# Expert weights as 4 MB pair loads, with filler multiplications on TensorE, in a two-layer hybrid encoder

## What is computed

```python
def hier_moe(h, wg, bg, we, be, w1, w3, w2):       # per layer: 32 experts, 4 groups of 8
    gprob = softmax(t @ wg + bg); gval, gidx = top_k(gprob, 1)
    ...
    for e in range(MOE_EXPERTS):
        he = jax.nn.silu(t @ w1[e]) * (t @ w3[e])  # w1, w3: 1024 x 512
        y = y + gate[:, e:e + 1] * (he @ w2[e])    # w2: 512 x 1024
```

## Time and profile before

| | |
|---|---|
| median of 3 runs | 1262.14 us (1261.61 to 1263.18) |
| profiled execution, its own time | 1262.0 us |
| its span | 1260.1 us |
| mean granted TensorE clock | 0.924 of full speed |
| TensorE busy | 1001.1 us, 79% of the span |
| read from HBM | 457.13 MB, 364 GB/s over the span |

### The profile page before, as it was taken

How to read it: one execution, slowest core, us unless ns; L and a number is a source line. 1 busy time by engine, 2 the same in 40 slices (tenths; PEclk the granted TensorE clock), 3 DMA queues, 4 the chain that set the end, 5 groups by cost and what they waited for, 6 DMA issues and landing times.

```text
span 1260.1 us, 20742 instructions
## 1 busy us (share of the span) xinstructions
PE 1001.1 (79%) x8905; PEld 606.8 (48%) x8905; DVE 334.1 (27%) x992; ACT 178.8 (14%) x393; POOL 18.4 (1%) x20
## 2 busy tenths in 40 slices
PE   9999999757576766667999999999857576666665
PEld 6667466424242424333888775465424242423332
DVE  4895341101010110002747553241101010101001
ACT  2315130000000000001224561030000000000000
POOL 0121000000000000000000000000000000000000
PEclk9999999988887988888999999999979887989889
DMA  9931599999999999999944546679999999999998
GB/s 377 416 135 67 226 400 429 428 427 431 426 430 427 430 427 430 428 428 426 409 171 168 184 151 273 261 294 427 426 430 427 430 427 430 428 430 428 430 426 334
DMA packets 34656, 458.91 MB, mean 364 GB/s; under 512 B 3856, under 2 KB 4656, under 8 KB 7216
## 3 DMA queue, kind: packets, MB, share of 16 engines
q1 hardware_dynamic: 33408, 454.00, 86.2%
q10 hardware_dynamic: 1200, 4.23, 1.0%
HBM read 457.13 MB, written 1.08 MB: 364 GB/s over the span
## 4 chain that ended last, share of the span: by engine, by line
DMA 39%; PE 35%; SPq 16%; DVE 2%; issue 1%; another core or an unknown queue 0%; ACT 0%; DVEq 0%
DMA extra<-in_moe_units 20%; DMA ring<-in_moe_units 19%; SPq L341 16%; PE bank L793 11%; PE bank L685 6%; PE bank L895 4%; PE bank L704 3%; PE bank L598 2%; PE bank L664 1%; PE bank L422 1%; PE bank L716 1%; PE bank L852 1%; PE bank L561 1%; PE bank L643 1%; PE bank L630 1%
## 5 line engine op out<-in xcount | busy, mean ns | idle before, releaser
L685 PE MATMUL bank<-ring,xT 128*32 128x256 f32 x2560 | 185.3, 437 | 83.4 <-DMA ring<-in_moe_units 83.4
L685 PE MATMUL bank<-extra,xT 128*32 128x256 f32 x1536 | 123.5, 475 | 71.8 <-DMA extra<-in_moe_units 71.8
L685 PEld LDWEIGHTS bank<-ring,xT 128*32 128x32 f32 x2560 | 84.4, 119 | 169.1 <-DMA ring<-in_moe_units 96.8
L793 PE MATMUL bank<-h,ring 128*128 128x256 f32 x576 | 130.1, 382 | 0.0
L793 PEld LDWEIGHTS bank<-h,ring 128*128 128x128 f32 x576 | 107.4, 190 | 16.5 <-issue 2.9
L685 PEld LDWEIGHTS bank<-extra,xT 128*32 128x32 f32 x1536 | 53.1, 128 | 128.4 <-DMA extra<-in_moe_units 84.9
L704 PE MATMUL bank<-ring,gates_ 128*32 128x256 f32 x1024 | 73.2, 434 | 42.6 <-DMA ring<-in_moe_units 42.6
L704 PE MATMUL bank<-extra,gates_ 128*32 128x256 f32 x1024 | 71.2, 425 | 35.8 <-DMA extra<-in_moe_units 33.4
L1575 DVE TENSOR_TENSOR hT<-hT,bank 128x128 f32<-128x128 f32 x64 | 18.4, 288 | 254.6 <-ACT hT L1065 254.6
L1065 ACT ACTIVATE hT<-bank 128x128 f32<-128x128 f32 x64 | 17.7, 277 | 449.0 <-PE bank L685 449.0
L716 PE MATMUL bank<-xT,gates_ 128*128 128x256 f32 x256 | 70.2, 407 | 3.8 <-DVE xT L1580 2.2
(11 more groups left out here) (312 smaller groups left out, 899.8 us busy)
## 6 DMA issues: line engine op xcount, KB each, us to landing
ring<-in_moe_units SPq DMA_DIRECT2D x112, 2048.0 KB, 49.1
extra<-in_moe_units SPq DMA_DIRECT2D x80, 2048.0 KB, 49.3
ring<-in_od_in_units SPq DMA_DIRECT2D x10, 2048.0 KB, 32.6
ring<-in_ev_in_units SPq DMA_DIRECT2D x5, 2048.0 KB, 26.5
ring<-in_od_out_units SPq DMA_DIRECT2D x4, 2048.0 KB, 8.1
ring<-in_ev_out_units SPq DMA_DIRECT2D x2, 2048.0 KB, 28.4
hT<-sums ACTq DMA_DIRECT2D x4, 512.0 KB, 4.4
every<-sums ACTq DMA_DIRECT2D x4, 512.0 KB, 5.6
```

The costliest lines, as they stand in the source:

```text
L685: last = mm(bank[4 + e % 2][32 * j:32 * j + 32, 0:256], xT[:, 4 * part + k, CAP * e:CAP * e + CAP], w[:, k, :, 256 * (j // 2) + j % 2:256 ...
L793: last = mm(o, w[:, k, P * q:P * q + P], (h2 if u else hT)[:, k, :], start=(k == 0), stop=(k == KT - 1))
```

## The change

In the experts' loop on SyncE, which loads steps 2 to 7 of each layer, units 0 to 9 come as five pairs, each one issue of 128 partitions x 8192 floats (4 MB). In HBM a pair now lies partition by partition, 32 KB in a row. Units 10 and 11 stay alone. Steps 0 and 1 still load unit by unit, from the new layout: 16 KB rows that are 32 KB apart. A pair reports on the semaphore of its even unit, so that unit waits for both, and the odd one waits for nothing new. A pair is issued once both its units are used. To lie side by side, `extra3` and `extra4` are cut from one tile, `extra2` and `extra0` from another, and units change places; `FREED` keeps the order in which places are filled in step 0. TensorE waits for `pt_ok` ahead of unit 2, no longer ahead of unit 8, and multiplies `ones` by itself: 18 times ahead of units 2, 4 and 6 in steps 1 to 7, 6 times ahead of quarter 2 and 4 times ahead of quarter 3, and in a layer's last step also 8 times ahead of quarter 0.

```diff
+UP_FILL, DOWN_FILL = (18, 0), (8, 0, 6, 4)
+PAIRS_UP = 5
-PLACES = [0, 1, 2, 3, 4, RING, RING + 1, RING + 2, RING + 3, 5, 6, RING + 4]
+PLACES = ([0, 1, 2, 3, RING + 2, RING, 5, 6, RING + 3, RING + 4, 4, RING + 1],
+          [0, 1, 2, 3, RING + 2, RING, 4, 5, RING + 3, RING + 4, RING + 1, 6])
+FREED = ([0, 1, 2, 3, 4, RING, RING + 1, RING + 2, RING + 4, 5, 6, RING + 3],
+         [0, 1, 2, RING, RING + 1, RING + 2, 3, 4, RING + 4, 5, 6, RING + 3])
+FIRST = [[PLACES[l].index(place) for place in FREED[l]] for l in range(2)]
...
+            def moe_pair(layer, pair, group):
+
+                sp.dma_start(pair_memory(layer, pair), pairw[layer, bass.ds(group, 1), pair, :, :, :].rearrange("g p w c -> (g p) (w c)")) \
+                    .then_inc(full[layer][moe_slot(layer, 2 * pair)], 16)
...
-                        sp.wait_ge(used[0], last_step * STEP_UNITS + PLACES.index(v) + 1)
+                        sp.wait_ge(used[0], last_step * STEP_UNITS + PLACES[0].index(v) + 1)
...
                 with sp.Fori(1, last_step) as i:
-                    for u in range(STEP_UNITS):
+                    for pair in range(PAIRS_UP):
+                        sp.wait_ge(used[layer], i * STEP_UNITS + 2 * pair + 2)
+                        moe_pair(layer, pair, (i + 1) % NGROUPS)
+                    for u in range(2 * PAIRS_UP, STEP_UNITS):
                         sp.wait_ge(used[layer], i * STEP_UNITS + u + 1)
                         moe_unit(layer, u, (i + 1) % NGROUPS)
...
+                    def landed(u):
+
+                        if u < 2 * PAIRS_UP and u % 2:
+                            pe.wait_ge(full[layer][moe_slot(layer, u)], moe_full(layer, u) + (0 if begin else 16))
+                        else:
+                            pe.wait_ge(full[layer][moe_slot(layer, u)], i * 16 + moe_full(layer, u))
...
+                    def up_later(e, part):
+
+                        if not begin:
+                            turnover(6, UP_FILL[part])
+                        up(e, part)
...
                         if q == 0:
-                            pe.wait_ge(m["pt_ok"], i + 1)
                             pe.wait_ge(m["ht_ok"], i * 4 + 4)
...
-                    up(1, 0)
+                    pe.wait_ge(m["pt_ok"], i + 1)
+                    up_later(1, 0)
                     turn(0)
-                    up(1, 1)
+                    up_later(1, 1)
...
                     if end:
                         for q in range(QUARTERS):
+                            turnover(6 + q % 2 if q else 6, DOWN_FILL[q])
                             down(q)
...
                         for q in range(1, QUARTERS):
+                            if not begin:
+                                turnover(6 + q % 2, DOWN_FILL[q] if q > 1 else 0)
                             down(q)
                             scatter(q - 1)
```

More of the change, by code:

```diff
@@ L133, in build @@
         con = sb("con", [P, C_KEEP])
-        extra3 = sb("extra3", [P, UNIT])
-        extra4 = sb("extra4", [P, UNIT])
+        extra34 = sb("extra34", [P, 2 * UNIT])
+        extra3, extra4 = extra34[:, 0:UNIT], extra34[:, UNIT:2 * UNIT]
         x = extra3[:, 0:2048].rearrange("p (a d) -> p a d", a=NT)
@@ L314, in moe_slot @@
         def moe_slot(layer, u):
-            place = PLACES[u]
+            place = PLACES[layer][u]
             return place if place >= RING else slot_of(layer, MIX_UNITS[layer] + place)
@@ L321, in moe_memory, with pair_memory @@
             return (extra0, extra1, extra2, extra3, extra4)[slot - RING][:, :] if slot >= RING else ring[:, slot, :]
+        def pair_memory(layer, pair):
+            slot = moe_slot(layer, 2 * pair)
+            if slot >= RING:
+                return (extra20 if slot == RING + 2 else extra34)[:, :]
+            return ring[:, slot:slot + 2, :].rearrange("p s c -> p (s c)")
         def moe_full(layer, u):
@@ L339, in moe_unit @@
             def moe_unit(layer, u, group):
-                sp.dma_start(moe_memory(layer, u), moew[layer, bass.ds(group, 1), u, :, :].rearrange("g p c -> (g p) c")) \
-                    .then_inc(full[layer][moe_slot(layer, u)], 16)
+                if u < 2 * PAIRS_UP:
+                    src = pairw[layer, bass.ds(group, 1), u // 2, :, u % 2, :]
+                else:
+                    src = lonew[layer, bass.ds(group, 1), u - 2 * PAIRS_UP, :, :]
+                sp.dma_start(moe_memory(layer, u), src.rearrange("g p c -> (g p) c")).then_inc(full[layer][moe_slot(layer, u)], 16)
+            def moe_pair(layer, pair, group):
+                sp.dma_start(pair_memory(layer, pair), pairw[layer, bass.ds(group, 1), pair, :, :, :].rearrange("g p w c -> (g p) (w c)")) \
+                    .then_inc(full[layer][moe_slot(layer, 2 * pair)], 16)
             cut = WORDS[0][0] // 2
@@ L680, in up @@
                         u = 2 * e + part
-                        pe.wait_ge(full[layer][moe_slot(layer, u)], i * 16 + moe_full(layer, u))
+                        landed(u)
                         w = moe_memory(layer, u).rearrange("p (w k f) -> p k w f", k=4, w=2)
@@ L1889, in expert_units @@
     units[:, :, UPS:] = downs.reshape(layers, NGROUPS, QUARTERS, P, UNIT)
-    return units
+    pairs = units[:, :, 0:2 * PAIRS_UP].reshape(layers, NGROUPS, PAIRS_UP, 2, P, UNIT).transpose(0, 1, 2, 4, 3, 5)
+    return pairs, units[:, :, 2 * PAIRS_UP:]
 def small_rows(w):
@@ L1919 @@
     whole = {n: np.asarray(inputs[n]) for n in _INPUTS}
+    moe_pairs, moe_lone = expert_units(whole["moe_w1"], whole["moe_w3"], whole["moe_w2"])
     packed = [("ev_in_units", in_units(whole["ev_w_in"][0], EVEN)), ("ev_out_units", out_units(whole["ev_w_out"][0], OUT_BLOCKS[0])),
               ("od_in_units", in_units(whole["od_w_in"][0], ODD)), ("od_out_units", out_units(whole["od_w_out"][0], OUT_BLOCKS[1])),
-              ("small", small_rows(whole)), ("x_cols", whole["x"][0].reshape(S, KT, P).transpose(2, 1, 0)), ("moe_units", expert_units(whole["moe_w1"], whole["moe_w3"], whole["moe_w2"]))]
+              ("small", small_rows(whole)), ("x_cols", whole["x"][0].reshape(S, KT, P).transpose(2, 1, 0)), ("moe_pairs", moe_pairs), ("moe_lone", moe_lone)]
     for name, a in [(n, whole[n]) for n in _INPUTS if n not in PACKED] + packed + [("con", con), ("lvl", lvl)]:
```

12 lines of the change are left out of this document (6 added, 6 removed).

## The result

The changed kernel took 1268.64 us (median of 5 runs, 1266.02 to 1270.43), the kernel before 1262.14: ratio **1.0051, interval 1.004 to 1.0063**, so slower by half a per cent. The profiled execution took 1266.02 us, the lowest of the five, with a span of 1264.1.

What follows compares the result with a forecast made beforehand. The prediction took DMA to bound the loops and TensorE to set the layers' ends. Packets -4.3, layer 1's end +2.9 and layer 0's +3.6 gave +2.2 us on 1262.0, so 1264.2 us; 8-in-10 range 1258.5 to 1269.5.

Steps and rivals of the forecast that it cites:

- What bounds the loops: Experts' loops: DMA engines fully busy at 425 to 428 GB/s, 58.7 us a step; only moving the bytes faster wins time.
- Fewer, longer packets: Loop loads: 32 KB rows as one packet, 8 fewer per engine and pair, 9 ns each, 60 pairs: -4.3 us.
- the first rival: Loop loads: 32 KB rows are cut into 16 KB packets, gaining only 0.4 us; total 1268.1 us; chance 0.22.
- the third: Loop loads: the fixed part goes with the issue, so pairs lose all of it: -8.6 us, total 1259.9; chance 0.23.
- The end of each layer: Last steps: quarters 0 to 3 and fillers run in a chain behind unit 9's landing: +3.6 us layer 0, +2.9 layer 1.
- The lower bound of the term: Both layers' ends together: +4.4 us if the fillers cost nothing.
- The clock at the pair's landing: Last steps: TensorE idles before unit 9 lands, so quarter 0 runs at the lower level, +1.35 us a layer: 1266.9; chance 0.10.
- Inside the loop: Loop steps: 64 fillers, 13.4 us on top of 39.4, fit into 58.7 us, and later pair issues cost nothing: 0.
- Edits that cost nothing: Units' new places, waits behind the loop and `pt_ok` ahead of unit 2: no cost while the queue holds loads.
- 1% of the 820 us of loops: Loop loads: rows 32 KB apart are read more slowly, +8 us, total 1272; chance 0.05.
- the likeliest case, no measurable change: Whole kernel: a time within about 0.2%, 2.5 us, of the kernel before; chance 0.41.
- the slower side: Whole kernel: slower than the kernel before by more than about 0.2%; chance 0.35.

Runs made afterwards that it cites:

- e6_change_again: The changed kernel itself, run again later beside other kernels on one chip: 1266.37 us, ratio 1.004.
- e12_short_packets: The changed kernel with its 4 MB issues, but all loads from the old layout, so each row is 16 KB: 1270.66 us, ratio 1.0074.
- e11_hold_clock: `e3_bare_end` with 18 fillers instead of 8 ahead of quarter 0 in each layer's last step: 1260.36 us, ratio 0.9986.
- e7_last_single_no_fill: The changed kernel with each layer's last step loaded unit by unit and no fillers anywhere: 1259.77 us, ratio 0.998.
- e5_last_single_bare: The changed kernel with each layer's last step loaded unit by unit and no fillers ahead of that step's quarters: 1259.67 us, ratio 0.9986.
- e9_rows_apart: The kernel before, loads and places unchanged, with only the new weight layout, so rows of units 0 to 9 are 32 KB apart: 1263.47 us, ratio 1.0011.
- e2_single: The changed kernel with all loads unit by unit again; its fillers, places and layout stay: 1263.14 us, ratio 1.0008.
- e3_bare_end: The changed kernel without the 6 and 4 fillers ahead of quarters 2 and 3 in each layer's last step: 1261.82 us, ratio 1.0005.

## Why the prediction was right or wrong

- **What bounds the loops: right.** The DMA share is 1.00 and the time of a step fell as the rate rose: the loop's quarters 0 started, each at its landing, at 346.06, 404.44, 462.80 and 521.15, so 58.36 us apart, as forecast (58.3 to 58.4). PEclk was 0.97.
- **Fewer, longer packets, -4.3 us: right.** 7680 fewer packets with data, 431 GB/s, and a step shorter by 58.75 - 58.36 = 0.39 us. Each engine saves 40 packets in it, so that is 10 ns for one, where the prediction had 9, and 4.7 us in all. The 4.3 us between the medians of `e6_change_again` and `e12_short_packets` fit too, but each of their intervals is about 0.14% either way, so the match to the decimal is luck. That throws out the first rival (packets don't get longer) and the third (the fixed part goes with the issue). The Trainium skill (DMA: Bandwidth & Descriptors, Bandwidth) has about 3 fabric cycles; by the prediction's estimate from that the gain would have been 1.7 us, and here the trace disagrees.
- **The end of each layer, +6.5: right, in mechanism and size.** Quarters 0 to 3 run back to back with no wait; layer 0 took 13.68 us for the forecast 13.7, layer 1 of `e6_change_again` 1255.06 - 1242.32 = 12.74 for 12.7. A filler took 0.216 us for 0.21. Loading the last step by units won 6.8, or 7.6 with the 0.8 of its ten lost pairs, low clocks at quarter 0 included. The lower bound of the term was miscounted: without the fillers' 2.1 us in each of the two layers 6.5 leaves 2.3, not 4.4, and what pairs cost without fillers came out at 3.0.
- **The clock at the pair's landing: a rival that came, in some executions.** "The 8 fillers lie in the time before" was the argument against it, and that argument failed: they end 1.5 to 4 us too early. Profiled executions show both outcomes, the lower level in 2 of 10, which by the rival's 1.35 us would be 0.5 us on average; `e11_hold_clock` puts 1.5 us on it. The rival's +2.7 for both layers is what an execution pays that has it twice.
- **Inside the loop, 0: right.** `e7_last_single_no_fill` and `e5_last_single_bare` differ by 0.1 us. The fillers cost nothing there and win nothing. TensorE is busy for 47.7 us of a step and not 52.8: the prediction laid the fillers on top of 39.4 us, a part of which ran at the lower level and no longer does.
- **"Edits that cost nothing": not shown to be nothing.** The paragraph named places and waits, and gave the new distance between the rows of single loads no price; the distance stood among the rivals as 1% of the 820 us of loops. In the loops it costs nothing (428 GB/s in `e9_rows_apart`). In all, that kernel is 1.6 us above the kernel before, with 0.3 to 2.5 as interval, and `e2_single` 1.5; in both traces the end of layer 0 ran in part at the lower clock, 3.46 and 3.64 us for quarters of 1.93 in the one and 3.62 us for 8 fillers in the other. How much of it is the layout's stays open.

With what the runs show for each term, the sum is -4.7 (packets) + 7.6 (ends, the clock at quarter 0 included) + 1.6 (`e9_rows_apart`) = **+4.5 us**, where the prediction had +2.2. Measured were +4.7 (`e6_change_again`) and +6.5 (the first measurement). The last two terms come from medians that are known to a microsecond or two, so that this fits the second measurement says little. The measured time is inside the prediction's range, and the two large terms were right; the forecast of 1264.2 was still 4.4 us too low, and the likeliest case, no measurable change, was not what came; the slower side had 0.35. What the sum left out are the clock at quarter 0 and whatever `e2_single` and `e9_rows_apart` share. Why the change's first five runs lie 2.3 us above the six later ones is open: their intervals, 1.004 to 1.0063 and 1.0025 to 1.0054, overlap, and single executions of it range over 7 us, where those of the kernel before mostly stay within 2.

One thing more of layer 1 was not forecast: the landing of unit 9 should have moved to 1243.93 + 0.75 - 2.15 = 1242.5 by the layer's late start and half of the packets' gain, and came at 1243.42. In the records the 16 completions of the last unit of this execution come between 1248.32 and 1252.72, 4.4 us apart, and a load is landed only with the last of its 16. The spread is not the pairs' own: it was 2.0 us in the kernel before and 4.0 in `e7_last_single_no_fill`, whose last step has single loads. Whether it delayed unit 9 here was not tested.

## What to carry to other kernels

Merging transfers pays by the packets it makes longer. At a place where compute ends behind the last landing it makes the first half wait for the second, one unit's transfer time; what the compute behind it can't absorb is the price, here about 3.0 us for two layers without fillers and 7.6 with them. So keep merged loads in the steady stream and load the last step in small pieces. Multiplications that only hold the clock belong ahead of a wait and should nearly reach the landing; behind it each costs its full length, and where transfers set the pace they win nothing at all. If such fillers stand on the chain, its shares don't tell the bound: take them out and look at the time. And before a small difference between two medians is given a cause, look at whether the traced execution is a typical one, and whether the place with the cause is also the place where its time is lost.

## What was not expected of the hardware

- Ahead of step 1's first loads the transfers are slow in the kernel before too, although the engines look busy: it moved 370 GB/s from 175 to 180 us at a DMA share of 0.98, and 429 from 180 on. The cause is open. With rows 32 KB apart the steady loop lost nothing (428 GB/s in `e9_rows_apart`, as before). The Trainium skill (DMA: Bandwidth & Descriptors, Latency and other measured facts) has a loss that grows with the rows' distance, but its 207 GB/s at 512 KiB, which the prediction quotes, is for copies between HBM tensors, where it calls 214 the full rate; it is hardly a loss. No run here shows such distances.
- Quarter 0 after 2.85 us of idling ran at 1.93 us in layer 0 of the change and after 2.77 in both layers of `e12_short_packets`, but after 2.73 it took 3.13 in `e3_bare_end`, each time behind 8 fillers. The length of the idling alone does not tell which level comes. In `e11_hold_clock`, where it was 0.83 and 0.86 us, the upper level stayed both times.
